# Turn, routing and norm of a tile inside the next tile's products, and twelve early rounds of the token choice, in an encoder layer on one core

## The chip, the cores and the metric

The kernel is one program on one core of a Trainium2 chip. The metric is the device time of one execution in microseconds. The core has five engines with a queue each: PE (TensorE, matrix products into PSUM), DVE (VectorE), ACT (ScalarE), POOL (GpSimd) and SP (SyncE, which issues most transfers). They wait for each other through semaphores: an instruction counts one up when it is done, and a later one, usually on another engine, waits for a value.

## The reference, cut to what matters

Two sequences (1024 and 512 rows of 1024 values) go through an input norm and one layer:

```python
proj = jnp.einsum('bsd,df->bsf', x, w_in)
pool_out = _pool_mixer(proj[..., :o1], w_pool, pool_scale)
attn_out = _mla(...)                                  # 8 heads, softmax attention
mix = jnp.einsum('bsm,md->bsd', jnp.concatenate([pool_out, attn_out], axis=-1), w_o)
x = _layer_norm(DEEPNORM_ALPHA * x + mix, ln1_g, ln1_b)
aff = jax.nn.softmax(jnp.einsum('td,de->te', xt, w_router), axis=-1)
gate, idx = lax.top_k(aff.T, cap)                     # 16 experts, cap 128 and 64 tokens
h = jax.nn.silu(xe @ w_gate) * (xe @ w_up);  ye = (h @ w_down) * gate
x = _layer_norm(DEEPNORM_ALPHA * x + scatter_add(ye), ln2_g, ln2_b)
```

Each expert takes the tokens that have the highest affinity to it, so no expert can start before the affinities of all tokens of a sequence are known.

## The kernel before, in words

Four stages follow each other: projection (0 to 217 us of the span), attention (217 to 575), mixing (575 to 796) and experts with the last norm (from 796). Between stages all engines meet. Inside a stage the order on each engine is the order in which the code is written; nothing reorders it.

**Attention** starts with blocks of keys and queries. On VectorE, `maximum(0, 0)` (L1005, the row maximum of the first scores) stands behind a wait for `u_stored`: the last store of uT must have left the buffer that later takes the heads' outputs (`divide`, L1028). Behind the first maximum comes `rotate(0, 1)` (L995), which needs the second half of the table of angles, `q_table`.

**Mixing** takes twelve tiles of 128 rows, eight of them of the long sequence. Every engine runs `step(s)` for s = 0 to 13; s = 2 to 5 are a hardware loop. For tile s, PE makes `pool_product` (w_pool, into the PSUM bank `ps_t[0]`) a step ahead, and eight `output_slices`, six products of 512 columns each, into `ps_mix[s % 2]`. VectorE adds the residual (L1638, counted by `summed`), takes mean and variance (L1642, L1648), and with the deviation from POOL (L1481, L1483) subtracts and scales (L1650), then multiplies by the gain (L1653). POOL adds the bias (L1487, counted by `x1_done`). ACT writes the scaled copy `acc` (L1532). PE turns the finished rows into `ps_t` (L1790) at the end of step s + 1, when the next tile's slices are done, and routes them (L1761) in step s + 2 behind four slices. The logits are turned (L1776), a softmax runs over VectorE and ACT (L1624, L1535, L1627, L1630), the affinities are turned (L1796) and copied into the lists' rows (L1669).

The parts that PE multiplies are split in two numbers: ACT rounds (`mix_hi`, L1506 for attention's four slices, L1510 for the pool's), VectorE takes the rest (`mix_lo`, L1560 and L1565). The attention part is first scaled by the softmax sums (`scale_attention`, L1556). The turn of a tile's rows waits for three counts: `x1_done`, `t_copied`, and `pool_lo_done` of the tile ahead, as the pool product uses the same bank.

**The token choice** finds a list's values eight at a time: a round is a maximum of eight (L1593), their replacement (L1598) and their positions (L1601). `EARLY_TOPK` gives, per step, how many rounds of the long sequence run ahead (before, after) of the norm; `JOIN`, ten, is their sum. Then come wide rounds for all lists and narrow ones for the short sequence (`PROMPT_FIRST`), in all `JOIN` + 8. VectorE copies positions and values into `lists` (L1700, L1702), PE turns them, and the choice of both halves is merged.

**Experts**: for each of 16 experts PE turns four pairs of gathered rows (L2252), ACT and VectorE split them (`x_lo_done`), and `gate_up` starts once all four pairs are split (L2268).

Of the kernel before, what the change touches and what calls it, by code (L numbers as in the profile page):

```python
# [18 lines left out]
P = 128  # L19
D = 1024  # L20
S_SAMPLE, S_PROMPT = 1024, 512
# [640 lines left out]
def phase_attention(nc, ident, dram, late, handed):  # L662

    with ExitStack() as ctx:
# [305 lines left out]
        def _(dve):  # L970
# [72 lines left out]
            dve.wait_ge(late.u_stored, 16 * N_TILES // 2)  # L1043
# [261 lines left out]
def phase_mix(nc, ident, dram, route, experts, late, first_rows):  # L1305

    with ExitStack() as ctx:
# [53 lines left out]
        topk_step, lists_turned, lists_copied = m.sem("c_topk_step"), m.sem("c_lists_turned"), m.sem("c_lists_copied")  # L1361
        merge_step, half_known = m.sem("c_merge_step"), m.sem("c_half_known")
# [138 lines left out]
        def _(act):  # L1501
# [17 lines left out]

            def step(s, slot=None):  # L1520
# [12 lines left out]
                if has(s, 2):  # L1533
                    act.wait_ge(r_max_done, s - 1)
                    act.activation(e_logits[:, :], ps_a[:, 0:N_EXPERTS], ACT.Exp, bias=neg_max[:, :],  # L1535
                                   accum_out=e_sum[:, :]).then_inc(r_exp_done, 1)
                if has(s, 1):
                    for h in range(2):
                        if has(s, 2):
# [3 lines left out]
                                       ACT.Copy).then_inc(t_copied, 1)  # L1543

            steps(act, step)
            act.wait_ge(wo_done, N_TILES)
            for c in range(experts.EARLY):
                act.wait_ge(experts.loaded[c], 16)
                act.activation(experts.hi[c][:, :], experts.raw[c], ACT.Copy).then_inc(experts.hi_done, 1)

        @block.vector
        def _(dve):
# [54 lines left out]
            def early_topk(s, part):  # L1607
                if isinstance(s, int) and s in EARLY_TOPK:
                    if part == 1 and s == N_TILES - 3:
# [5 lines left out]
            def step(s, slot=None):  # L1615
                slot = s % 2 if slot is None else slot
                if has(s, -1) and not (isinstance(s, int) and s + 1 >= N_TILES):
                    rest_attention(s + 1, 1 - slot)
                    rest_pool(s + 1, 1 - slot)
                early_topk(s, 0)  # L1620
# [4 lines left out]
                if has(s, 2):  # L1625
# [4 lines left out]
                    nc.vector.tensor_scalar(affinity[:, rows_of(s - 2)], e_logits[:, :], e_inv[:, :], None, ALU.mult).then_inc(r_aff_done, 1)  # L1630
                if has(s, 0):
# [11 lines left out]
                    if not isinstance(s, int) or s >= 2:  # L1643
# [5 lines left out]
                    dve.wait_ge(rstd_done, s + 1)  # L1649
                    nc.vector.tensor_scalar(x1[:, slot, :], x1[:, slot, :], moments[:, slot, 0:1], rstd[:, slot:slot + 1],  # L1650
                                            ALU.subtract, ALU.mult).then_inc(centred, 1)
                    dve.wait_ge(centred, s + 1)
                    nc.vector.tensor_tensor(x1[:, slot, :], x1[:, slot, :], ln_g[:, :], ALU.mult).then_inc(scaled, 1)  # L1653
                    if isinstance(s, int) and s == N_TILES - 1:
                        dve.wait_ge(x1_done, s)
                        dve.wait_ge(scaled, s + 1)
                        nc.vector.tensor_tensor(x1[:, slot, :], x1[:, slot, :], ln_b[:, :], ALU.add).then_inc(x1_done, 1)
                if has(s, 2):
                    dve.wait_ge(aff_turned, s - 1)
                    rows = rows_of(s - 2)  # L1660
                    if rows == quarter(0):
                        to = affT[rows, bass.ds((s - 2) * P, P)]
                    elif rows == quarter(1):
                        at = (s - 2) * P - HALF_SAMPLE
                        to = affT[rows, at:at + P]
                    else:
                        at = (s - 2 - SAMPLE_TILES) % 2 * P
                        to = left[(JOIN - 1) % 2][rows, at:at + P]
                    nc.vector.tensor_copy(to, ps_a[rows, P:2 * P]).then_inc(aff_copied, 1)  # L1669
# [17 lines left out]
            found = slice(PROMPT_FIRST, PROMPT_FIRST + CAP_PROMPT)  # L1687
            for x, source in enumerate((index, value)):
                for part in range(4):
                    rows = quarter(part)  # L1690
                    got = source[rows, 0:CAP_SAMPLE] if part < 2 else source[rows, found]
                    if part % 2:
                        got = got[:, ::-1]
                    to = lists[rows, x, :]
                    if part >= 2:
                        got = got.unsqueeze(1).to_broadcast([N_EXPERTS, 2, CAP_PROMPT])
                        to = to.rearrange("p (a c) -> p a c", a=2)
# [706 lines left out]
```

## Time and profile before

| what | value |
|---|---|
| time, median of 3 runs | 1306.43 us (1303.58 to 1306.99) |
| profiled execution, its own time | 1306.65 us |
| its span, first to last instruction | 1304.8 us |
| busy PE / DVE / ACT / POOL | 1169.1 / 921.6 / 687.1 / 377.1 us |
| mean granted clock of PE | 0.96 of full speed |

The table's busy times are sums over the whole span, and the stages have different limits: a full engine in one stage says nothing of the next. In rows of a timeline the columns are the start and the length in microseconds, the engine, the line of the kernel, the instruction with what it writes and reads, its shape and how many were merged; a bracket at the end gives how long the engine had been idle and what released it.

### The profile page before, as it was taken

The numbers are of one execution on the slowest core, as the hardware profiler recorded it, in microseconds if no ns is written. First come the engines' busy times: TensorE is split into PE (matmuls) and PEld (weight loads), VectorE is DVE, ScalarE is ACT, GpSimd is POOL, SyncE is SP. The second block draws the span as 40 slices with busy tenths as digits, with TensorE's granted clock in tenths as the row PEclk, the third lists the DMA queues.
The fourth block names the chain that finished last, engine by engine and source line by source line (L and its number), as shares of the span: only waits on it lengthen the run. The fifth ranks groups of instructions, "written<-read, shape, count | busy, mean of one in ns | idle before, by whom it ended". The sixth has DMA issues, their size and how long they took to land. (4 is left out here: it accounts for less than half of the span.)

```text
span 1304.8 us, 21729 instructions
## 1 busy us (share of the span) xinstructions
PE 1169.1 (90%) x7322; PEld 1054.1 (81%) x7322; DVE 921.6 (71%) x1538; ACT 687.1 (53%) x1191; POOL 377.1 (29%) x437
## 2 busy tenths in 40 slices
PE   5999998789999999989999925999999999999960
PEld 4999997678888888877888715999999999999950
DVE  7655534587877788776566884777777777777738
ACT  4222223566666666662222233667766666776636
POOL 1322210256430000002222132333444343334317
PEclk9999999999999999989999956999999999999985
DMA  8244476832321013038555715888888888888738
GB/s 302 87 165 164 147 240 224 252 119 87 96 64 50 8 35 118 13 107 236 180 162 168 252 65 187 264 274 273 261 280 276 271 289 278 266 255 283 209 83 335
DMA packets 161363, 242.24 MB, mean 186 GB/s; under 512 B 13248, under 2 KB 123424, under 8 KB 161312
## 3 DMA queue, kind: packets, MB, share of 16 engines
q1 hardware_dynamic: 151456, 206.97, 47.4%
q0 software_dynamic: 9856, 34.61, 10.1%
q8 instruction: 29, 0.48, 0.1%
q14 instruction: 22, 0.18, 0.0%
HBM read 179.37 MB, written 62.18 MB: 185 GB/s over the span
## 5 line engine op out<-in xcount | busy, mean ns | idle before, releaser
L2263 PE MATMUL ps_gate_up<-xT_hi_lo,w_hi 128*128 128x384 f32 x896 | 262.9, 357 | 1.4 <-DVE xT_hi_lo L2192 1.4
L2264 PE MATMUL ps_gate_up<-xT_hi_lo,w_lo 128*128 128x192 f32 x896 | 225.2, 251 | 0.0
L2264 PEld LDWEIGHTS ps_gate_up<-xT_hi_lo,w_lo 128*128 128x128 f32 x896 | 171.6, 192 | 0.6
L2263 PEld LDWEIGHTS ps_gate_up<-xT_hi_lo,w_hi 128*128 128x128 f32 x896 | 169.6, 189 | 2.4 <-issue 1.7
L2187 DVE TENSOR_TENSOR w_lo<-w_raw,w_hi 128x2048 fp32r<-128x2048 f32 x63 | 143.8, 2282 | 0.0
L1005 DVE TENSOR_REDUCE neg_max<-ps_scores 128x1 f32<-128x1024 f32 (+1 forms) x80 | 97.7, 1221 | 49.2 <-PE ps_scores L76 48.5
L905 ACT ACTIVATE pT_hi<-ps_probsT 128x512 fp32r<-128x512 f32 x160 | 87.1, 596 | 72.6 <-PE ps_probsT L1134 72.2
L2127 ACT ACTIVATE w_hi<-w_raw 128x2048 fp32r<-128x2048 f32 x62 | 118.4, 1910 | 0.0
L2044 POOL TENSOR_TENSOR d_wait_carrier<-d_zero 128x1 f32<-128x1 f32 x78 | 37.3, 478 | 274.2 <-PE ps_xT L2253 144.7
L1017 DVE TENSOR_TENSOR pT_lo<-ps_probsT,pT_hi 128x512 fp32r<-128x512 f32 x160 | 101.5, 674 | 4.4 <-ACT pT_hi L905 4.3
L914 ACT ACTIVATE probs<-ps_scores,neg_max 128x1024 f32<-128x1024 f32 (+1 forms) x96 | 93.5, 979 | 20.6 <-DVE neg_max L1005 20.3
L1134 PEld LDWEIGHTS ps_probsT<-ident,probs 128*128 128x128 f32 x640 | 73.5, 141 | 29.8 <-DVE pT_lo L1017 14.2
L1134 PE MATMUL ps_probsT<-ident,probs 128*128 128x128 f32 x640 | 84.8, 276 | 14.0 <-ACT probs L914 10.8
L74 PE MATMUL ps_mix<-w_hi,mix_hi 128*128 128x512 f32 x192 | 79.9, 416 | 2.6 <-DVE mix_lo L1565 1.4
L76 PE MATMUL ps_mix<-w_hi,mix_lo 128*128 128x512 f32 x192 | 76.6, 399 | 0.0
L75 PE MATMUL ps_mix<-w_lo,mix_hi 128*128 128x512 f32 x192 | 76.5, 398 | 0.0
L74 PE MATMUL ps_scores<-k_hi,w_in_hi_then_latents 128*128 128x512 f32 x160 | 64.9, 406 | 4.3 <-DVE w_in_lo_then_latents L999 3.1
L2187 DVE TENSOR_TENSOR w_lo<-hen_windows_then_w_o_raw,w_hi 128x2048 fp32r<-128x2048 f32 x30 | 68.6, 2285 | 0.0
L75 PE MATMUL ps_scores<-k_lo,w_in_hi_then_latents 128*128 128x512 f32 x160 | 63.4, 396 | 0.0
L76 PE MATMUL ps_scores<-k_hi,w_in_lo_then_latents 128*128 128x512 f32 x160 | 63.0, 394 | 0.0
L2209 DVE TENSOR_TENSOR hen_windows_then_w_o_raw<-ps_gate_up,gate_rest 128x192 f32<-128x192 f32 x64 | 22.9, 357 | 56.3 <-ACT gate_rest L2144 54.2
L76 PE MATMUL ps_lat<-w_in_hi_then_latents,x0T_lo 128*128 128x384 f32 (+1 forms) x192 | 61.4, 320 | 0.0
(311 smaller groups left out, 3246.5 us busy)
## 6 DMA issues: line engine op xcount, KB each, us to landing
w_raw<-in_w_down SPq DMA_DIRECT2D x32, 1024.0 KB, 6.2
hen_windows_then_w_o_raw<-in_w_gate SPq DMA_DIRECT2D x16, 1024.0 KB, 5.4
hen_windows_then_w_o_raw<-in_w_up SPq DMA_DIRECT2D x16, 1024.0 KB, 5.4
w_raw<-in_w_gate SPq DMA_DIRECT2D x16, 1024.0 KB, 10.3
w_raw<-in_w_up SPq DMA_DIRECT2D x16, 1024.0 KB, 9.2
scratch_x<-x SPq DMA_DIRECT2D x24, 512.0 KB, 2.7
scratch_v<-v_out SPq DMA_DIRECT2D x12, 512.0 KB, 5.8
v_hi_lo<-scratch_v SPq DMA_DIRECT2D x8, 768.0 KB, 4.7
```

The lines of the kernel that those rows point to most:

```text
L74: nc.tensor.matmul(out, a_hi, b_hi, start=first, stop=False)
L75: nc.tensor.matmul(out, a_hi, b_lo, start=False, stop=False)
L76: return nc.tensor.matmul(out, a_lo, b_hi, start=False, stop=last)
L905: act.activation(pT_hi[unit % 2][half_place(n, h)], ps_t[h][:, :].rearrange("p (k t) -> p k t", t=P), ACT.Copy).then_inc(t_hi_done, 1)
L914: last = act.activation(probs[:, n % 2, x * width:(x + 1) * width], ps_s[n % 2][:, x * width:(x + 1) * width], ACT.Exp, bias=neg_max[:, n ...
L1005: nc.vector.tensor_reduce(neg_max[:, n % 2, 0:count], ps_s[n % 2][:, :].rearrange("p (x c) -> p x c", x=count), op=ALU.max, axis=AX.X, neg ...
L1017: nc.vector.tensor_tensor(pT_lo[unit % 2][at], ps_t[h][:, :].rearrange("p (k t) -> p k t", t=P), f32(pT_hi[unit % 2][at]), ALU.subtract).t ...
L1134: last = nc.tensor.transpose(ps_t[h][:, k * P:(k + 1) * P], probs[:, n % 2, (4 * h + k) * P:(4 * h + k + 1) * P], ident[:, :])
L2127: act.activation(w_hi[c][:, :], raw[c], ACT.Copy).then_inc(hi_done, 1)
L2187: nc.vector.tensor_tensor(w_lo[c][:, :], raw[c], f32(w_hi[c][:, :]), ALU.subtract).then_inc(lo_done, 1)
L2263: nc.tensor.matmul(ps[:, 0:2 * N], w_hi[chunk][:, at], xT[:, k, :], start=k == 0, stop=False)
L2264: nc.tensor.matmul(ps[:, 0:N], w_lo[chunk][:, at], xT[:, k, 0:N], start=False, stop=False)
```

## The change: what it does

- Attention: the wait for `u_stored` moves from ahead of the first maximum to the first `divide`.
- Mixing, PE: the turn of a tile's rows moves forward, behind the sixth slice of the next tile; routing (behind the seventh) and the turn of the logits follow in the same step instead of the next one. The turn of the affinities moves to behind the fourth slice.
- Mixing, VectorE: the softmax of a tile comes first in a step, then the rests of the next tile's two parts, then the copy of the affinities, then the early rounds, then the norm.
- Norm: VectorE subtracts the mean and multiplies by the gain in one instruction that doesn't need the deviation; ACT multiplies by the deviation; POOL adds the bias as before. In the last tile VectorE does the last two in one instruction.
- Token choice: three early rounds in each of steps 9 to 12, ahead of the sum; twelve in place of ten. ACT copies the four parts of the values into the lists.
- ACT splits the first two weight chunks of the first expert in step 12 instead of after the steps.
- Experts: the first gate product waits for each pair where it is used, not for all four.

```diff
                 b = unit // 2
+                if unit == 0:
+                    dve.wait_ge(late.u_stored, 16 * N_TILES // 2)
...
             rest_keys(0, (1, 2))
-            dve.wait_ge(late.u_stored, 16 * N_TILES // 2)
 
...
-        EARLY_TOPK = {N_TILES - 3: (0, 2), N_TILES - 2: (1, 2), N_TILES - 1: (1, 1), N_TILES: (0, 3), N_TILES + 1: (0, 0)}
+        EARLY_TOPK = {N_TILES - 3: (3, 0), N_TILES - 2: (3, 0), N_TILES - 1: (3, 0), N_TILES: (3, 0), N_TILES + 1: (0, 0)}
         JOIN = sum(a + b for a, b in EARLY_TOPK.values())
         PROMPT_FIRST = 8 * JOIN
-        TOPK_STEPS = 3 * (JOIN + PROMPT_ROUNDS) - 1 + 8
+        TOPK_STEPS = 3 * (JOIN + PROMPT_ROUNDS) - 1 + 4
...
                 if has(s, 2):
-                    act.wait_ge(logits_done, s - 1)
-                    act.activation(logitsT[:, :], ps_r[:, 0:P], ACT.Copy).then_inc(logits_copied, 1)
+                    act.wait_ge(r_max_done, s - 1)
+                    act.activation(e_logits[:, :], ps_a[:, 0:N_EXPERTS], ACT.Exp, bias=neg_max[:, :],
+                                   accum_out=e_sum[:, :]).then_inc(r_exp_done, 1)
+                if has(s, 1) and not (isinstance(s, int) and s == N_TILES):
+                    act.wait_ge(rstd_done, s)
+                    act.wait_ge(centred, s)
+                    act.activation(x1[:, 1 - slot, :], x1[:, 1 - slot, :], ACT.Copy, scale=rstd[:, 1 - slot:2 - slot]).then_inc(scaled, 1)
+                if isinstance(s, int) and s == N_TILES:
+                    for c in range(2):
+                        split_expert(c)
...
-                if has(s, 2):
-                    act.wait_ge(r_max_done, s - 1)
-                    act.activation(e_logits[:, :], ps_a[:, 0:N_EXPERTS], ACT.Exp, bias=neg_max[:, :],
-                                   accum_out=e_sum[:, :]).then_inc(r_exp_done, 1)
...
+                    act.wait_ge(logits_done, s)
+                    act.activation(logitsT[:, :], ps_r[:, 0:P], ACT.Copy).then_inc(logits_copied, 1)
...
+            for c in range(2, experts.EARLY):
+                split_expert(c)
+            act.wait_ge(topk_step, TOPK_STEPS - 4 - 1)
+            for part in range(4):
+                act.activation(list_row(1, part), found_in(value, part), ACT.Copy).then_inc(values_listed, 1)
...
-                if has(s, -1) and not (isinstance(s, int) and s + 1 >= N_TILES):
-                    rest_attention(s + 1, 1 - slot)
-                    rest_pool(s + 1, 1 - slot)
-                early_topk(s, 0)
...
+                if has(s, -1) and not (isinstance(s, int) and s + 1 >= N_TILES):
+                    rest_attention(s + 1, 1 - slot)
+                    rest_pool(s + 1, 1 - slot)
+                if has(s, 2):
+                    dve.wait_ge(aff_turned, s - 1)
...
+                    nc.vector.tensor_copy(to, ps_a[rows, P:2 * P]).then_inc(aff_copied, 1)
+                early_topk(s, 0)
...
-                    dve.wait_ge(rstd_done, s + 1)
-                    nc.vector.tensor_scalar(x1[:, slot, :], x1[:, slot, :], moments[:, slot, 0:1], rstd[:, slot:slot + 1],
-                                            ALU.subtract, ALU.mult).then_inc(centred, 1)
-                    dve.wait_ge(centred, s + 1)
-                    nc.vector.tensor_tensor(x1[:, slot, :], x1[:, slot, :], ln_g[:, :], ALU.mult).then_inc(scaled, 1)
+                    dve.wait_ge(stats_done, s + 1)
+                    nc.vector.scalar_tensor_tensor(out=x1[:, slot, :], in0=x1[:, slot, :], scalar=moments[:, slot, 0:1], in1=ln_g[:, :],
...
-                        nc.vector.tensor_tensor(x1[:, slot, :], x1[:, slot, :], ln_b[:, :], ALU.add).then_inc(x1_done, 1)
...
+                        dve.wait_ge(rstd_done, s + 1)
+                        dve.wait_ge(centred, s + 1)
+                        nc.vector.scalar_tensor_tensor(out=x1[:, slot, :], in0=x1[:, slot, :], scalar=rstd[:, slot:slot + 1], in1=ln_b[:, :],
+                                                       op0=ALU.mult, op1=ALU.add).then_inc(x1_done, 1)
...
-                    pe.wait_ge(t_copied, 2 * (s - 1))
-                    for k in range(KD):
...
+                    pe.wait_ge(r_aff_done, s - 1)
+                    rows = slice(0, rows_of(s - 2).stop)
+                    nc.tensor.transpose(ps_a[rows, P:2 * P], affinity[:, rows], ident[:, :]).then_inc(aff_turned, 1)
...
-                if has(s, 2):
-                    pe.wait_ge(aff_copied, s - 2)
...
                 if has(s, 1):
                     pe.wait_ge(x1_done, s)
...
-                if has(s, 2):
-                    pe.wait_ge(r_aff_done, s - 1)
-                    rows = slice(0, rows_of(s - 2).stop)
-                    nc.tensor.transpose(ps_a[rows, P:2 * P], affinity[:, rows], ident[:, :]).then_inc(aff_turned, 1)
+                if has(s, 0):
+                    output_slices(s, slot, range(6, 7))
...
+                if has(s, 1):
+                    pe.wait_ge(t_copied, 2 * s)
+                    for k in range(KD):
...
+                if has(s, 0):
+                    output_slices(s, slot, range(7, KD)).then_inc(wo_done, 1)
+                if has(s, 1):
+                    if not isinstance(s, int) or s >= 2:
+                        pe.wait_ge(aff_copied, s - 1)
+                    pe.wait_ge(logits_copied, s)
+                    nc.tensor.matmul(ps_a[:, 0:N_EXPERTS], logitsT[:, :], add_groups[:, :], start=True, stop=True).then_inc(logits_turned, 1)
...
+            pe.wait_ge(values_listed, 4)
...
+                    if e is not None and k < 4:
+                        pe.wait_ge(x_lo_done, 4 * e + k + 1)
...
-                pe.wait_ge(x_lo_done, 4 * e + 4)
...
-                    gate_or_up(ps_g, GATE[f // 2], f, g_done)
+                    gate_or_up(ps_g, GATE[f // 2], f, g_done, e if f == 0 else None)
```

Where this puts the work is shown by the order of instructions on two engines. A row gives the line, the operation, what it writes and reads, its shape and, in brackets, the semaphores that it waits for. Semaphores are numbers that each stage uses anew, and a row may give one the name that it had in an earlier stage: `a_filled` is here `r_aff_done`, `a_kv_stored` is `aff_copied`, `a_kr_stored` is `aff_turned`.

First PE around step 10 of mixing (`ps_x1T` is the bank `ps_t`, in which the rows are turned, and `x1T` its copy, `ps_affinity` the bank of the turned logits and affinities). Before, from the end of the tile ahead to the routing and the turn of the logits:

```order
L74 MATMUL ps_mix<-w_hi,mix_hi 128x512 [waits c_summed,c_mix_lo_done]
...
L1761 MATMUL ps_router<-x1T,w_router 32x128 [waits c_t_copied]
...
L1728 MATMUL ps_x1T<-d,aw_then_windows_then_w_o_raw 128x128 [waits c_d_loaded1]
...
L74 MATMUL ps_mix<-w_hi,mix_hi 128x512 [waits c_logits_copied,a_kv_stored]
...
L1776 MATMUL ps_affinity<-add_groups,logitsT 128x16
...
L1790 MATMUL ps_x1T<-ident,x 128x128 [waits c_pool_lo_done,c_t_copied,c_x1_done]
...
L1796 MATMUL ps_affinity<-ident,affinity 80x128 [waits a_filled]
```

Now:

```order
L74 MATMUL ps_mix<-w_hi,mix_hi 128x512 [waits c_summed,c_mix_lo_done]
...
L1777 MATMUL ps_affinity<-ident,affinity 80x128 [waits a_filled]
L1745 MATMUL ps_x1T<-d,aw_then_windows_then_w_o_raw 128x128 [waits c_d_loaded1]
...
L1792 MATMUL ps_x1T<-ident,x 128x128 [waits c_pool_lo_done,c_t_copied,c_x1_done]
...
L1804 MATMUL ps_router<-x1T,w_router 32x128 [waits c_t_copied]
...
L1813 MATMUL ps_affinity<-add_groups,logitsT 128x16 [waits c_logits_copied,a_kv_stored]
```

Before, the turn of the rows closes a step, and their routing comes a step later behind four slices. Now the rows are turned behind the sixth slice of the next tile, routed behind the seventh, and their logits turned behind the eighth, all in one step; the turn of the affinities comes behind four slices in place of the step's end.

Next VectorE in that step. Before, from the early rounds to the copy of the affinities:

```order
L1630 TENSOR_SCALAR affinity<-e_logits,e_inv 128x16 [waits a_kr_stored,c_r_inv_done]
L1638 SCALAR_TENSOR_TENSOR x<-x_again,ps_mix 128x1024 [waits c_x0_loaded1,c_x1_stored1,c_wo_done,c_acc_done,c_t_done]
...
L1648 BN_AGGR ln_moments<-ln_stats 128x2
L1650 TENSOR_SCALAR x<-x,ln_moments,ln_rstd 128x1024 [waits c_rstd_done]
L1653 TENSOR_TENSOR x<-x,ln_g_all 128x1024 [waits c_centred]
L1669 COPY affT_sample<-ps_affinity 16x128 [waits a_kr_stored]
L1556 TENSOR_TENSOR mix_raw<-mix_raw,inv_rows 128x512 [waits c_inv_loaded1,c_mix_loaded1]
L1593 MAX topk_value<-affT_sample 48x8 [waits a_kv_stored]
...
L1560 TENSOR_TENSOR mix_lo<-mix_raw,mix_hi 128x512 [waits c_mix_hi_done]
L1565 TENSOR_TENSOR mix_lo<-ps_x1T,mix_hi 128x512 [waits c_pool_hi_done]
```

Now:

```order
L1647 TENSOR_REDUCE router_neg_max<-ps_affinity 128x1 [waits c_r_exp_done,c_logits_turned]
...
L1653 TENSOR_SCALAR affinity<-e_logits,e_inv 128x16 [waits a_kr_stored,c_r_inv_done]
L1587 TENSOR_TENSOR mix_lo<-mix_raw,mix_hi 128x512 [waits c_mix_hi_done]
L1592 TENSOR_TENSOR mix_lo<-ps_x1T,mix_hi 128x512 [waits c_pool_hi_done]
L1668 COPY affT_sample<-ps_affinity 16x128 [waits a_kr_stored]
L1620 MAX topk_value<-affT_sample 48x8 [waits a_kv_stored]
...
L1677 SCALAR_TENSOR_TENSOR x<-x_again,ps_mix 128x1024 [waits c_x0_loaded1,c_x1_stored1,c_wo_done,c_acc_done,c_t_done]
...
L1687 BN_AGGR ln_moments<-ln_stats 128x2
L1689 SCALAR_TENSOR_TENSOR x<-x,ln_moments,ln_g_all 128x1024 [waits c_stats_done]
L1583 TENSOR_TENSOR mix_raw<-mix_raw,inv_rows 128x512 [waits c_inv_loaded1,c_mix_loaded1]
```

Softmax and copy now stand ahead of the early rounds and of the sum, the norm has one instruction over the tile in place of two, and nothing but the scaling of the next attention part follows it.

## Rows read from the trace of the kernel before

**Rows 1.** Windows, mid mixing: busy us of PE, PEld, DVE, ACT, POOL; clock.

```profile
656.00:670.00 14.00, 14.00 (x85) 11.34 (x83) 8.22 (x15) 3.91 (x8) 3.72 (x4) 1.00 0.54 169
```

**Rows 2.** Timeline of PE, one tile: start us, length us, engine, line, instruction.

```profile
663.52 1.03 PE L1790 MATMUL ps_x1T<-ident,x 128*128 128x128 f32 x8
...
664.42 0.48 PE L74 MATMUL ps_mix<-w_hi,mix_hi 128*128 128x512 f32 x1
...
670.07 0.64 PE L1761 MATMUL ps_router<-x1T,w_router 128*32 128x128 f32 x16
670.64 1.16 PE L1728 MATMUL ps_x1T<-d,hen_windows_then_w_o_raw 128*128 128x128 f32 x8
671.55 0.47 PE L74 MATMUL ps_mix<-w_hi,mix_hi 128*128 128x512 f32 x1
```

**Rows 3.** Timeline of DVE in the same tile and into the next.

```profile
663.82 1.22 DVE L1638 SCALAR_TENSOR_TENSOR x<-x_again,ps_mix 128x1024 f32<-128x1024 f32 x1 [0.54 <-PE ps_mix L76]
...
666.40 0.20 DVE L1648 BATCH_NORM_AGGREGATE ln_moments<-ln_stats 128x2 f32<-128x12 f32 x1
...
669.73 0.67 DVE L1556 TENSOR_TENSOR mix_raw<-mix_raw,inv_rows 128x512 f32<-128x512 f32 x1
671.61 1.59 DVE L1560 TENSOR_TENSOR mix_lo<-mix_raw,mix_hi 128x512 fp32r<-128x512 f32 x1 [1.20 <-ACT mix_hi L1506]
673.12 0.68 DVE L1565 TENSOR_TENSOR mix_lo<-ps_x1T,mix_hi 128x512 fp32r<-128x512 f32 x1
676.09 0.17 DVE L1624 TENSOR_REDUCE router_neg_max<-ps_affinity 128x1 f32<-128x16 f32 x1 [2.30 <-PE ps_affinity L1776]
...
676.90 0.23 DVE L1630 TENSOR_SCALAR affinity<-e_logits,e_inv 128x16 f32<-128x16 f32 x1
```

**Rows 4.** Timeline of POOL there, the bias of two tiles.

```profile
669.69 2.95 POOL L1487 TENSOR_TENSOR x<-x,ln_b_all 128x1024 f32<-128x1024 f32 x1 [2.19 <-DVE x L1653]
...
683.67 2.37 POOL L1487 TENSOR_TENSOR x<-x,ln_b_all 128x1024 f32<-128x1024 f32 x1 [2.19 <-DVE x L1653]
```

**Rows 5.** Timeline of ACT there, one pass over a tile.

```profile
672.74 1.06 ACT L1532 ACTIVATE acc_out<-x 128x1024 f32<-128x1024 f32 x1 [0.30 <-POOL x L1487]
```

**Rows 6.** Timeline of DVE in the expert stage, a split of weights.

```profile
844.05 2.28 DVE L2187 TENSOR_TENSOR w_lo<-w_raw,w_hi 128x2048 fp32r<-128x2048 f32 x1
```

**Rows 7.** Timeline of POOL then, a one-element operation.

```profile
844.56 1.83 POOL L2044 TENSOR_TENSOR d_wait_carrier<-d_zero 128x1 f32<-128x1 f32 x1 [6.33 <-DMA scratch_acc<-y_prompt_rows,scatter_at]
```

**Rows 8.** Timeline of DVE, the sums of tiles 0, 1, 8 and 11.

```profile
596.71 1.21 DVE L1638 SCALAR_TENSOR_TENSOR x<-x_again,ps_mix 128x1024 f32<-128x1024 f32 x1
...
608.47 1.22 DVE L1638 SCALAR_TENSOR_TENSOR x<-x_again,ps_mix 128x1024 f32<-128x1024 f32 x1 [1.86 <-PE ps_mix L76]
...
705.39 1.22 DVE L1638 SCALAR_TENSOR_TENSOR x<-x_again,ps_mix 128x1024 f32<-128x1024 f32 x1 [0.54 <-PE ps_mix L76]
...
750.45 1.22 DVE L1638 SCALAR_TENSOR_TENSOR x<-x_again,ps_mix 128x1024 f32<-128x1024 f32 x1 [0.35 <-PE ps_mix L76]
```

**Rows 9.** Timeline of DVE, last softmax to the lists.

```profile
768.40 0.17 DVE L1624 TENSOR_REDUCE router_neg_max<-ps_affinity 128x1 f32<-128x16 f32 x1
...
770.32 0.70 DVE L1593 MAX8 topk_value<-topk_left 112x8 f32<-112x512 f32 x1
...
782.68 0.42 DVE L1593 MAX8 topk_value<-topk_left 48x8 f32<-48x256 f32 x1
...
783.95 0.42 DVE L1593 MAX8 topk_value<-topk_left 48x8 f32<-48x256 f32 x1
...
785.92 0.97 DVE L1700 COPY topk_lists<-topk_value 16x128 f32<-16x128 f32 x4
```

**Rows 10.** Timeline of DVE at the start of attention.

```profile
233.65 1.22 DVE L1005 TENSOR_REDUCE neg_max<-ps_scores 128x1 f32<-128x1024 f32 x1 [5.87 <-PE ps_scores L76]
238.73 0.69 DVE L995 TENSOR_TENSOR q_work<-ps_q,q_table 128x512 f32<-128x512 f32 x1 [3.86 <-DMA q_table<-in_q_table]
```

**Rows 11.** Timeline of PE at the first expert's first product.

```profile
801.00 0.66 PE L2263 MATMUL ps_gate_up<-xT_hi_lo,w_hi 128*128 128x384 f32 x1 [1.36 <-DVE xT_hi_lo L2192]
```

More of the change, by code:

```diff
@@ L1368, in phase_mix, with found_in, list_row @@
         ROUNDS, PROMPT_ROUNDS = CAP_SAMPLE // 8, CAP_PROMPT // 8
-        EARLY_TOPK = {N_TILES - 3: (0, 2), N_TILES - 2: (1, 2), N_TILES - 1: (1, 1), N_TILES: (0, 3), N_TILES + 1: (0, 0)}
+        EARLY_TOPK = {N_TILES - 3: (3, 0), N_TILES - 2: (3, 0), N_TILES - 1: (3, 0), N_TILES: (3, 0), N_TILES + 1: (0, 0)}
         JOIN = sum(a + b for a, b in EARLY_TOPK.values())
         PROMPT_FIRST = 8 * JOIN
-        TOPK_STEPS = 3 * (JOIN + PROMPT_ROUNDS) - 1 + 8
+        TOPK_STEPS = 3 * (JOIN + PROMPT_ROUNDS) - 1 + 4
+        def found_in(source, part):
+            rows = quarter(part)
+            got = source[rows, 0:CAP_SAMPLE] if part < 2 else source[rows, PROMPT_FIRST:PROMPT_FIRST + CAP_PROMPT]
+            if part % 2:
+                got = got[:, ::-1]
+            return got if part < 2 else got.unsqueeze(1).to_broadcast([N_EXPERTS, 2, CAP_PROMPT])
+        def list_row(x, part):
+            to = lists[quarter(part), x, :]
+            return to if part < 2 else to.rearrange("p (a c) -> p a c", a=2)
         block = ctx.enter_context(nc.Block())
@@ L1518, in _, with split_expert @@
                     round_attention(0, 0)
+            def split_expert(c):
+                act.wait_ge(wo_done, N_TILES)
+                act.wait_ge(experts.loaded[c], 16)
+                act.activation(experts.hi[c][:, :], experts.raw[c], ACT.Copy).then_inc(experts.hi_done, 1)
             def step(s, slot=None):
@@ L1608, in early_topk @@
                 if isinstance(s, int) and s in EARLY_TOPK:
-                    if part == 1 and s == N_TILES - 3:
+                    if part == 0 and s == N_TILES - 3:
                         dve.wait_ge(aff_copied, SAMPLE_TILES)
@@ L1630, in step @@
                     nc.vector.tensor_scalar(affinity[:, rows_of(s - 2)], e_logits[:, :], e_inv[:, :], None, ALU.mult).then_inc(r_aff_done, 1)
+                if has(s, -1) and not (isinstance(s, int) and s + 1 >= N_TILES):
[3 more added lines that the diff above has]
+                    dve.wait_ge(aff_turned, s - 1)
+                    rows = rows_of(s - 2)
+                    if rows == quarter(0):
+                        to = affT[rows, bass.ds((s - 2) * P, P)]
+                    elif rows == quarter(1):
+                        at = (s - 2) * P - HALF_SAMPLE
+                        to = affT[rows, at:at + P]
+                    else:
+                        at = (s - 2 - SAMPLE_TILES) % 2 * P
+                        to = left[(JOIN - 1) % 2][rows, at:at + P]
+                    nc.vector.tensor_copy(to, ps_a[rows, P:2 * P]).then_inc(aff_copied, 1)
+                early_topk(s, 0)
                 if has(s, 0):
@@ L1686, in _ @@
             dve.wait_ge(topk_step, n)
[L1687 to L1697, printed above, removed]
-                    start = (0, HALF_SAMPLE, S_SAMPLE, S_SAMPLE + HALF_PROMPT)[part]
-                    if x or not part:
-                        nc.vector.tensor_copy(to, got).then_inc(topk_step, 1)
-                    else:
-                        nc.vector.tensor_scalar(to, got, float(start), None, ALU.add).then_inc(topk_step, 1)
-            assert n + 8 == TOPK_STEPS
+            for part, first_token in enumerate((0, HALF_SAMPLE, S_SAMPLE, S_SAMPLE + HALF_PROMPT)):
+                to, got = list_row(0, part), found_in(index, part)
+                if part == 0:
+                    nc.vector.tensor_copy(to, got).then_inc(topk_step, 1)
+                else:
+                    nc.vector.tensor_scalar(to, got, float(first_token), None, ALU.add).then_inc(topk_step, 1)
+            assert n + 4 == TOPK_STEPS
             dve.wait_ge(lists_turned, 1)
@@ L1769, in step @@
                     output_slices(s, slot, range(4, 6))
-                if has(s, 2):
-                    pe.wait_ge(aff_copied, s - 2)
-                    pe.wait_ge(logits_copied, s - 1)
-                if has(s, 0):
-                    output_slices(s, slot, range(6, 7))
-                if has(s, 2):
-                    nc.tensor.matmul(ps_a[:, 0:N_EXPERTS], logitsT[:, :], add_groups[:, :], start=True, stop=True).then_inc(logits_turned, 1)
-                if has(s, 0):
-                    output_slices(s, slot, range(7, KD)).then_inc(wo_done, 1)
-                if isinstance(s, int) and s == 1:
-                    pe.wait_ge(ln_loaded, 48)
-                    pe.wait_ge(groups_step, GROUPS - 1)
                 if has(s, 1):
```

32 lines of the change are left out of this document (10 added, 22 removed).

## The prediction

> **What bounds the kernel now.** I read the windows first. In the middle of the mixing stage PE is busy for all 14.00 us of a 14 us stretch at full clock, VectorE for 8.22, ScalarE for 3.91, GpSimd for 3.72 [rows 1]. So between tile 1 and tile 8 a tile costs what PE's products cost: seven tiles from 608.47 to 705.39, 13.85 us each [rows 8]. Then I read the timelines of one tile, since the change moves waits and not work. PE turns the finished rows of the tile before right behind a tile's last product (663.52), and routes them only after four slices of the following tile (670.07) [rows 2]. That leaves nearly a tile for the norm, the bias and the softmax. The end of the stage is the reverse: from the last tile's sum at 750.45 to the first joint round of the token choice at 770.32, and on to the lists, VectorE decides [rows 8, 9]. In the expert stage PE is the bound again, and it waits once, 1.36 us before its first product [rows 11].
>
> **The change part by part.** Times T below count from a tile's sum on VectorE (663.82 in the trace).
>
> *VectorE's early wait.* The first row maximum of attention starts at 233.65 after 5.87 us of idling, which is put down to PE; the wait for the stored uT that the change moves stands just there. But next VectorE rotates a query block, and that waits 3.86 us for the q_table load, until 238.73 [rows 10]. The second maximum stands behind this rotation in both kernels, and the load hangs on nothing that VectorE does. The first maximum then comes 5.6 us sooner and the queue stops at the same 238.73. Bounds 0 and -5.6; I take 0.
>
> *The loop, where the turn moves forward.* The new PE order asks for three things inside a tile: the affinities after four slices; the finished rows after six; and, as the transposes share a PSUM bank with the pool product, the rest of the next tile's pool part. No engine has more work, so the cost is what comes late.
>
> The affinities: statistics end at T 2.78 (666.60), the new fused product at 1.22 (the sum's length, same form) brings 4.0, scaling the attention part 0.67 brings 4.7, and softmax from maximum to affinities takes 1.04 (676.09 to 677.13) [rows 3]; with handovers, T 5.85. PE starts the tile at T -0.3 and needs 5.65 us for four slices (664.42 to 670.07), plus a small turn of the logits [rows 2]: ready at 5.5. It waits about 0.4.
>
> The transposes: ScalarE's new scaling stands behind the softmax's exponential in its queue, so it starts at about 5.4 and ends, at 1.06 for a pass [rows 5], at 6.5. Its reader is the bias on GpSimd: 2.37 us when undisturbed [rows 4], so to 8.9. Now VectorE's rest of the attention part becomes ready near 7.1 and falls inside the bias. In the trace that meeting is seen: the bias ran 669.69 to 672.64 [rows 4], the rest started at 671.61, took 1.59 and ended 0.56 after the bias, where the same size of two SBUF inputs took 0.67 [rows 3]. So the rest ends at 9.5, the pool part's rest 0.6 later, and PE has its permission at 10.2. Without any of this PE would be there at 5.5 + 0.91 for the pool product (670.64 to 671.55) + 2.83 for two slices [rows 2] = 9.25. The two waits are one sum, as the second swallows the first: 0.95. One more thing lengthens it: GpSimd's two small operations for the deviation start beside the fused product, which reads two SBUF tensors. A one-element operation took 1.83 us on GpSimd while such a product ran, and ended with it [rows 6, 7]. Held behind the product and the scaling, the deviation comes near 5.5 and shifts the scaling by up to 0.25. Bounds 0.4 and 1.2 per tile; I take 1.0, seven times: +7.0 (2.8 to 8.4).
>
> The page "SBUF — State Buffer" of the Trainium skill, section "Who interferes with whom", has a rule that speaks against this change: a VectorE instruction with two SBUF inputs and a GpSimd instruction that reads SBUF exclude each other, and whichever was issued second blocks for all of the first. The trace agrees, with the 1.59 for 0.67 and the 1.83 above. By that rule the loop's term is the +7.0; if the engines only shared, it would be the +2.8.
>
> *Tile 1.* Before, from the sum of tile 0 to that of tile 1 are 11.76 us [rows 8], since nothing is turned or routed in it. Now both are: 0.90 (663.52 to 664.42) and 0.57 (670.07 to 670.64) [rows 2], 1.5 in all, and a wait at the transposes, where PE is ready at 8.95 and the permission comes between 8.75 and 10.3. +2.8 (1.5 to 2.9).
>
> *Three early rounds in each of tiles 9 to 12.* A round costs 2.06 us: six take from 770.32 to 782.68 [rows 9]. Three stand behind the pool part's rest and ahead of the next sum, so a tile lasts 10.15 + 0.3 for the copy + 6.2 = 16.6, and VectorE is the bound. For the last one nothing is left to scale: the affinities are early, rows are finished at 8.6, then 0.9 + 1.4 + 0.6 + 1.4 + 0.3 of PE give 13.2. Together 46.4 against 45.06 from tile 8 to tile 11 [rows 8]: +1.3 (0.9 to 1.8).
>
> *From the last sum to the joint rounds.* Before 19.87. Now the second fused product ends at 4.0 + 0.85 of waiting for the deviation + 1.2 = 6.1; softmax, turn and copy of tile 10 take 1.92 (768.40 to 770.32) [rows 9], three rounds 6.2, and again 1.92: 16.1. ScalarE rounds two chunks in the meantime (four passes' worth, 4.2 us), then the tile's copies, so the routing is at most 0.7 late: 16.8. -3.1 (-2.0 to -3.8).
>
> *Rounds and lists.* Twelve early rounds for ten: four wide joint rounds in place of six, four narrow ones (1.27, 782.68 to 783.95) in place of two: -2 x (2.06 - 1.27) = -1.6. The four copies of values, 0.97 [rows 9], go to ScalarE, which starts them half a round earlier: -1.0 (0 to -1.0).
>
> *The first gate product* no longer waits for the fourth pair. PE's 1.36 [rows 11] go, since three pairs arrive while it works: -1.4 (-1.0 to -1.4). The three added waits per expert are long met and cost nothing, at most some hundredths each.
>
> Sum: 2.8 + 7.0 + 1.3 - 3.1 - 1.6 - 1.0 - 1.4 = +4.0. The profiled execution took 1306.65 us for a span of 1304.8, 0.2 above the median of 1306.43, so I add it to the execution: 1310.7. All lower ends together give -2.6 (the early wait apart), all upper ends +8.5.
>
> **The rivals.** *VectorE is not held* (the other side): the rest of the attention part runs beside the bias. It decides if its record has its 0.67 although the bias is running. Then only the 0.4 for the affinities stays per tile (+2.8), tile 1 costs 1.5, a tile with rounds 7.1 + 0.67 + 0.6 to the end of the pool part's rest, then 0.3 + 6.2, 14.9 in all, so 43.0 for the last three, -2.1, and with the -7.1 of the end: -4.9, 1301.8. Against it stands [rows 3, 4]; for it, that the order of arrival could turn where tiles slip.
>
> *Half the wait*: the deviation isn't held, handovers are short, and a tile costs 0.5 more: +0.5, 1307.2. For it: my terms are a few tenths each.
>
> *No wait at all*: the affinities too are in time: -7.7, 1299. Against it: VectorE's queue of known durations.
>
> *The early wait is worth its 5.6*: then -1.6, 1305. Against it: the q_table load [rows 10].
>
> **How the numbers follow.** Forecast 0.53, own range 1309 to 1315, half the wait 0.22, not held 0.15, no wait 0.05, early wait 0.05. A measurement of this kernel can tell about 0.3% (3.9 us). The forecast lies just above that line, so 0.05 of it counts as no change: slower 0.48, same 0.32 (with half the wait and the early wait), faster 0.20. The range 1301 to 1316 leaves out the case without any wait and the upper tail.
>
> **What would show it.** Right: from tile 2 to tile 8 sums 14.6 to 15.1 us apart; PE idle ahead of the transposes with the pool part's rest as releaser, and ahead of the turned affinities; VectorE's rest of the attention part at 1.5 to 2.5 us, ending about 0.6 after the bias; sums of tiles 9 and 10 about 16.6 apart with VectorE never idle ahead of them; 16 to 17 from the last sum to the joint rounds; the second maximum of attention still right behind the q_table. Wrong: sums 13.9 apart, a rest of 0.7 under a running bias, or a second maximum before 238.

## The result, and the profile after

The changed kernel took 1316.83 us (median of 4 runs, 1315.03 to 1319.82) against 1305.74 for the kernel before (4 runs, 1303.58 to 1306.99): a ratio of 1.0083, interval 1.0067 to 1.0100, so about 11 us slower. The profiled execution has a span of 1313.1 us and a time of 1315.03, 8.4 above that of before. The forecast of slower was right; the time lies 0.8 above its range.

The sums of tiles 0, 1, 8 and 11 on VectorE, as in [rows 8]:

```profile
596.20 1.21 DVE L1677 SCALAR_TENSOR_TENSOR x<-x_again,ps_mix 128x1024 f32<-128x1024 f32 x1
...
611.01 1.22 DVE L1677 SCALAR_TENSOR_TENSOR x<-x_again,ps_mix 128x1024 f32<-128x1024 f32 x1 [4.87 <-PE ps_mix L76]
...
714.28 1.22 DVE L1677 SCALAR_TENSOR_TENSOR x<-x_again,ps_mix 128x1024 f32<-128x1024 f32 x1 [4.59 <-PE ps_mix L76]
...
760.65 1.22 DVE L1677 SCALAR_TENSOR_TENSOR x<-x_again,ps_mix 128x1024 f32<-128x1024 f32 x1 [1.01 <-PE ps_mix L76]
```

Tile 1 takes 14.81 for 11.76, the seven tiles of the loop 14.75 each for 13.85, tiles 9 to 11 together 46.37 for 45.06. Next come the last softmax and the joint rounds, which answer [rows 9]. VectorE first:

```profile
774.92 0.17 DVE L1647 TENSOR_REDUCE router_neg_max<-ps_affinity 128x1 f32<-128x16 f32 x1 [0.18 <-PE ps_affinity L1813]
775.53 0.16 DVE L1650 RECIPROCAL e_inv<-e_sum 128x1 f32<-128x1 f32 x1 [0.43 <-ACT e_logits L1544]
775.72 6.98 DVE L1653 TENSOR_SCALAR affinity<-e_logits,e_inv 128x16 f32<-128x16 f32 x1
783.25 0.30 DVE L1668 COPY topk_left<-ps_affinity 16x128 f32<-16x128 f32 x1 [0.56 <-PE ps_affinity L1777]
783.59 0.69 DVE L1620 MAX8 topk_value<-topk_left 112x8 f32<-112x512 f32 x1
...
796.61 0.21 DVE L1717 CAST topk_lists<-topk_index 16x128 f32<-16x128 uint32 x1
```

And GpSimd, ScalarE and PE of the same stretch:

```profile
767.07 3.70 ACT L1538 ACTIVATE w_hi<-hen_windows_then_w_o_raw 128x2048 fp32r<-128x2048 f32 x2
...
769.05 9.17 POOL L1507 TENSOR_TENSOR w_lo<-hen_windows_then_w_o_raw,w_hi 128x2048 fp32r<-128x2048 f32 x2 [3.74 <-ACT w_hi L1538]
...
775.39 3.70 ACT L1538 ACTIVATE w_hi<-w_raw 128x2048 fp32r<-128x2048 f32 x2
...
778.11 4.56 POOL L1507 TENSOR_TENSOR w_lo<-w_raw,w_hi 128x2048 fp32r<-128x2048 f32 x1
...
782.75 0.46 PE L1777 MATMUL ps_affinity<-ident,affinity 128*112 128x128 f32 x1 [7.87 <-DVE affinity L1653]
797.63 0.69 PE L1819 MATMUL ps_router<-ident,topk_lists 128*128 128x128 f32 x2 [14.42 <-DVE topk_lists L1719]
...
810.07 0.67 PE L2283 MATMUL ps_gate_up<-xT_hi_lo,w_hi 128*128 128x384 f32 x1
```

The multiplication of 128x16 elements that makes the last affinities (L1653) took 6.98 us, where it took 0.23 in [rows 3]. It ended at 782.70, and the third of GpSimd's splits of the first expert's weights (L1507, two in the one row, one in the other) ended at 782.67. No other instruction of any engine ends there. Behind the multiplication stand PE, the copy and the joint rounds.

In the kernel before, the lists begin and are turned at

```profile
784.92 0.21 DVE L1700 CAST topk_lists<-topk_index 16x128 f32<-16x128 uint32 x1
...
786.94 0.69 PE L1801 MATMUL ps_router<-ident,topk_lists 128*128 128x128 f32 x2 [16.99 <-DVE topk_lists L1700]
```

Set against before by stretches of the two spans, in us:

| stretch | before | after | difference | predicted |
|---|---|---|---|---|
| start to the first sum | 596.71 | 596.20 | -0.5 | 0 |
| tile 1 | 11.76 | 14.81 | +3.05 | +2.8 |
| tiles 2 to 8 | 96.92 | 103.27 | +6.35 | +7.0 |
| tiles 9 to 11 | 45.06 | 46.37 | +1.3 | +1.3 |
| last sum to joint rounds | 19.87 | 22.94 | +3.1 | -3.1 |
| joint rounds | 14.60 | 13.02 | -1.6 | -1.6 |
| lists | 2.02 | 1.02 | -1.0 | -1.0 |
| turn of the lists to first gate product | 14.06 | 12.44 | -1.6 | -1.4 |
| from there to the end | 503.80 | 503.03 | -0.8 | 0 |
| sum | 1304.8 | 1313.1 | +8.3 | +4.0 |

Every term but one came out within 0.8 us. That one is off by 6.2. The table accounts for the 8.3 between the two profiled executions; the medians are 11.1 apart, in a repeat 8.4 (the last experiment), and where the other 2.7 lie isn't shown.

Inside the loop one tile shows the two waits. PE's turn of the affinities and of the rows [rows 2]:

```profile
645.50 0.39 PE L76 MATMUL ps_mix<-w_hi,mix_lo 128*128 128x512 f32 x1
646.09 0.28 PE L1777 MATMUL ps_affinity<-ident,affinity 128*16 128x128 f32 x1 [0.19 <-DVE affinity L1653]
...
649.67 0.39 PE L76 MATMUL ps_mix<-w_hi,mix_lo 128*128 128x512 f32 x1
650.27 1.09 PE L1792 MATMUL ps_x1T<-ident,x 128*128 128x128 f32 x8 [0.21 <-DVE mix_lo L1592]
```

VectorE's rest of the attention part, and GpSimd's bias, which answer [rows 3, 4]:

```profile
646.68 2.39 POOL L1502 TENSOR_TENSOR x<-x,ln_b_all 128x1024 f32<-128x1024 f32 x1 [1.79 <-ACT x L1549]
...
647.15 2.46 DVE L1587 TENSOR_TENSOR mix_lo<-mix_raw,mix_hi 128x512 fp32r<-128x512 f32 x1 [1.12 <-ACT mix_hi L1521]
649.54 0.68 DVE L1592 TENSOR_TENSOR mix_lo<-ps_x1T,mix_hi 128x512 fp32r<-128x512 f32 x1
```

The rest took 2.46 and ended at 649.61, 0.54 after the bias (649.07). Products follow each other here every 0.227 us, so PE was ready for the two turns at 645.73 and 649.90 and lost about 0.37 ahead of either.

At the start of attention [rows 10], the first maximum came 4.9 us sooner, and VectorE's queue stopped at the q_table load all the same:

```profile
228.77 1.22 DVE L1005 TENSOR_REDUCE neg_max<-ps_scores 128x1 f32<-128x1024 f32 x1
237.07 0.69 DVE L995 TENSOR_TENSOR q_work<-ps_q,q_table 128x512 f32<-128x512 f32 x1 [7.08 <-DMA q_table<-in_q_table]
237.68 1.21 DVE L1005 TENSOR_REDUCE neg_max<-ps_scores 128x1 f32<-128x1024 f32 x1
```

### The profile page after: what moved, and what is told of

It reads as the page before. It is cut to its first block and busy times, and to the rows that moved or that the text cites. A ratio compares the mean times of both kernels' runs of the same rounds, so it can differ in the third digit from the quotient of the medians.

```text
span 1313.1 us, 21797 instructions
## 1 busy us (share of the span) xinstructions
PE 1171.7 (89%) x7322; PEld 1051.5 (80%) x7322; DVE 925.8 (71%) x1532; ACT 699.8 (53%) x1206; POOL 385.5 (29%) x437
## 5 line engine op out<-in xcount | busy, mean ns | idle before, releaser
L2062 POOL TENSOR_TENSOR d_wait_carrier<-d_zero 128x1 f32<-128x1 f32 x78 | 40.0, 513 | 269.5 <-PE ps_xT L2271 141.7
```

## The experiments

Theory: two holds of VectorE by GpSimd make the loss, the small one in every tile and a large one at the last softmax, which the sum had not priced. Rivals: the stall is ScalarE's or a fetch of instructions; and the loop grows because PE's new order is longer by itself. Each ratio is to runs of the kernel before on the same chip, whose medians were 1307.67, 1308.54 and 1308.99.

**Take the stalled instruction off VectorE.** In ScalarE's last step, with VectorE's own multiplication of this tile left out:

```diff
+                    if isinstance(s, int) and s == N_TILES + 1:
+                        act.wait_ge(r_inv_done, s - 1)
...
+                        act.activation(affinity[:, rows_of(s - 2)], e_logits[:, :], ACT.Copy, scale=e_inv[:, :]).then_inc(r_aff_done, 1)
```

> The changed kernel, but the last tile's affinities (e_logits times e_inv) are computed by ScalarE behind its exponential; VectorE's multiplication of that tile is gone. Theory (VectorE's multiplication of two SBUF operands stood from 775.72 to 782.70 because GpSimd's three splits of the first expert's weights, 769.05 to 782.67, hold a port that it needs): the last softmax ends about 6.5 us sooner, 16.2 to 16.6 from the last sum to the joint rounds in place of 22.9, and the time falls from 1316.8 to about 1310.2. GpSimd's splits stay where they are. Rival (something else held VectorE there, say a fetch of instructions or ScalarE's split): the next VectorE instruction stands instead, and the time stays within 1 us of 1316.8.

Measured: 1310.62, ratio 1.0030 (1.0018 to 1.0043); last sum to joint rounds 16.27. ScalarE multiplies and VectorE goes on while GpSimd splits:

```profile
768.53 9.14 POOL L1507 TENSOR_TENSOR w_lo<-hen_windows_then_w_o_raw,w_hi 128x2048 fp32r<-128x2048 f32 x2 [3.73 <-ACT w_hi L1538]
...
775.22 0.31 ACT L1550 ACTIVATE affinity<-e_logits,e_inv 128x16 f32<-128x16 f32 x1 [0.23 <-DVE e_inv L1655]
...
776.08 0.30 DVE L1674 COPY topk_left<-ps_affinity 16x128 f32<-16x128 f32 x1 [0.89 <-PE ps_affinity L1783]
776.41 0.69 DVE L1625 MAX8 topk_value<-topk_left 112x8 f32<-112x512 f32 x1
...
777.61 4.55 POOL L1507 TENSOR_TENSOR w_lo<-w_raw,w_hi 128x2048 fp32r<-128x2048 f32 x1
```

The stall is gone and did not move to the next VectorE instruction, so a fetch of instructions is out.

**Leave the instruction, move GpSimd.**

```diff
             steps(pool, step)
+            pool.wait_ge(r_aff_done, N_TILES)
```

> The changed kernel, but GpSimd starts its splits of the first expert's weights only when the last tile's affinities are there; ScalarE's two early splits stay in step 12. Theory (GpSimd holds VectorE): the multiplication takes 0.23 again, the joint rounds begin 16.2 to 16.6 after the last sum, and GpSimd's 13.7 us end beside the end of the rounds; 1310.2, up to 1 us more if they meet the additions of the lists. Rival (ScalarE's split, which also ran then, holds VectorE): the multiplication still takes 3 to 7 us, and the time stays at 1313 to 1317.

Measured: 1311.37, ratio 1.0028 (1.0015 to 1.0040), 16.22 from the last sum to the joint rounds. The multiplication:

```profile
778.05 0.23 DVE L1654 TENSOR_SCALAR affinity<-e_logits,e_inv 128x16 f32<-128x16 f32 x1
...
778.37 9.01 POOL L1508 TENSOR_TENSOR w_lo<-hen_windows_then_w_o_raw,w_hi 128x2048 fp32r<-128x2048 f32 x2 [10.74 <-DVE affinity L1654]
787.35 4.50 POOL L1508 TENSOR_TENSOR w_lo<-w_raw,w_hi 128x2048 fp32r<-128x2048 f32 x1
```

ScalarE's splits ran where the change put them (one pair began at 777.72, ahead of the multiplication), so they are not the cause.

**Make the stall in the kernel before**, by ScalarE's early splits alone (`split_expert` holds the lines that stood behind the steps):

```diff
+                if isinstance(s, int) and s == N_TILES:
+                    for c in range(2):
+                        split_expert(c)
```

> The kernel before, with one edit of the change alone: ScalarE splits the first two weight chunks of the first expert at the end of step 12. Theory: GpSimd starts its splits about 763.7 in place of 770.85, so VectorE's last multiplication of the softmax (769.2) meets them; if GpSimd's instructions hold the port back to back it stands until the third ends near 777.4, +8 us, 1314; if the port comes free between two, until 772.8, +3.6, 1309.4. Rival (the stall needs the new order of VectorE or of the norm): no change, 1305.7.

Measured: 1311.44, ratio 1.0032 (1.0016 to 1.0048); last sum to joint rounds 23.15 for 19.87.

```profile
766.43 9.03 POOL L1492 TENSOR_TENSOR w_lo<-hen_windows_then_w_o_raw,w_hi 128x2048 fp32r<-128x2048 f32 x2 [9.39 <-ACT w_hi L1523]
...
771.99 3.51 DVE L1637 TENSOR_SCALAR affinity<-e_logits,e_inv 128x16 f32<-128x16 f32 x1
...
775.43 4.50 POOL L1492 TENSOR_TENSOR w_lo<-w_raw,w_hi 128x2048 fp32r<-128x2048 f32 x1
```

One edit of seven makes a stall in an otherwise unchanged kernel. Here VectorE came through at the border of the second and third split (775.46), the smaller of the two forecasts, though the time is 2 us above what was expected for it; in the changed kernel it was held across that border in two executions (6.98, 6.94), and in a variant of it below (6.94).

**Read the tensor from PSUM**, to see what is held. In the last tile ScalarE writes the exponentials there (its edit isn't shown), and VectorE's edit, its lines cut at the right, is

```diff
-                    nc.vector.tensor_scalar(affinity[:, rows_of(s - 2)], e_logits[:, :], e_inv...
+                    of = ps_a[:, 32:32 + N_EXPERTS] if isinstance(s, int) and s == N_TILES + 1 else e_logits[:, :]
+                    nc.vector.tensor_scalar(affinity[:, rows_of(s - 2)], of, e_inv...
```

> The changed kernel, but in the last tile ScalarE writes the exponentials into PSUM and VectorE's multiplication reads them there (its factor e_inv and its result stay in SBUF); GpSimd's and ScalarE's splits are where the change put them. Theory (what is held is a multiplication that reads its tensor from SBUF, as the Trainium skill's page on SBUF says of tensor_scalar in a mode of two ports): it takes 0.2 to 0.3 in the middle of GpSimd's split, 16.3 from the last sum to the joint rounds, about 6.5 us below the changed kernel (1310). Rival (the factor that is read from SBUF, or the write to SBUF, is what is held): it stands 6 to 7 us as before, 1316.8.

Measured: 1311.73, ratio 1.0022 (1.0005 to 1.0038), 16.2 from the last sum (760.93) to the joint rounds. In the middle of GpSimd's splits:

```profile
769.33 9.12 POOL L1507 TENSOR_TENSOR w_lo<-hen_windows_then_w_o_raw,w_hi 128x2048 fp32r<-128x2048 f32 x2 [3.73 <-ACT w_hi L1538]
...
776.01 0.23 DVE L1655 TENSOR_SCALAR affinity<-ps_affinity,e_inv 128x16 f32<-128x16 f32 x1
...
777.13 0.69 DVE L1621 MAX8 topk_value<-topk_left 112x8 f32<-112x512 f32 x1
...
778.36 4.57 POOL L1507 TENSOR_TENSOR w_lo<-w_raw,w_hi 128x2048 fp32r<-128x2048 f32 x1
```

The same multiplication with the same factor and result runs in 0.23. So its tensor in SBUF is what made it wait.

**The loop: no bias on GpSimd.** ScalarE's scaling and GpSimd's bias are gone; in their place stands, behind the softmax on VectorE, for the tile before:

```diff
+                    nc.vector.scalar_tensor_tensor(out=x1[:, 1 - slot, :], in0=x1[:, 1 - slot, :], scalar=rstd[:, 1 - slot:2 - slot], in1=ln_b[:, :],
+                                                   op0=ALU.mult, op1=ALU.add).then_inc(x1_done, 1)
```

> The changed kernel, but in every tile VectorE multiplies by the deviation and adds the bias in one instruction behind the softmax (as the changed kernel does in the last tile); ScalarE's scaling and GpSimd's bias are gone. Theory (in the loop the rest of the attention part stands 2.46 for 0.68 behind GpSimd's bias, and PE waits for it at the turn): the rest takes 0.68, sums of tiles 2 to 8 stand 14.0 to 14.3 apart in place of 14.75, tiles 9 and 10 about 15.4 in place of 16.6; together -5 to -7, with the stall of the last softmax left in: about 1310.5. Rival (the turn costs PE its time by itself, whatever VectorE does): sums stay 14.7 apart and only the last tiles gain 1 to 2 us, 1315.

Measured: 1305.96, ratio 0.9986 (0.9971 to 1.0002). In the trace the rest takes 0.68, the loop's tiles 14.31, tile 1 13.47 for 14.81, tiles 9 to 11 43.05 for 46.37, and PE's wait ahead of the rows' turn is gone. The stall of the last softmax stays:

```profile
659.60 0.68 DVE L1579 TENSOR_TENSOR mix_lo<-mix_raw,mix_hi 128x512 fp32r<-128x512 f32 x1
...
768.30 6.94 DVE L1645 TENSOR_SCALAR affinity<-e_logits,e_inv 128x16 f32<-128x16 f32 x1
```

These stretches fell by 7.8 together, where 5 to 7 had been expected, and the time lies 4.5 below the 1310.5 expected. The edit took work off the chain of the norm as well as the hold. The changed kernel's own trace tells the two apart: there the bias ended at 649.07, 0.83 before PE was ready for the rows' turn, so the rows were in time; VectorE's rests ended at 650.22, and PE began at 650.27.

**The end alone, on the kernel before**: the value lists on ScalarE and the waits of the gate pairs, as in the change's diff.

> The kernel before with two edits of the change alone: ScalarE copies the four parts of the values into the lists, and the first gate product waits for each pair where it is used. Theory (both are on the path behind the loop, and worth what the sum gave them): the stretch from the lists to the first gate product shortens by 1.0 + 1.4, the time falls by 2 to 2.7 us against the kernel before (ratio about 0.998). Rival (PE only waits later, at the weights or at the second pair): 0 to -1 us.

Measured: 1303.71, ratio 0.9966 (0.9946 to 0.9985); the lists 1.02 for 2.02, the turn to the gate product 12.42 for 14.06. Both terms are there without the rest of the change. The two stretches fell by 2.6; the time fell by more than the 2 to 2.7 expected, 4.8, with an interval from 2.0 to 7.1.

**Both holds away** (the bias on VectorE and the last affinities on ScalarE):

> The changed kernel without either hold by GpSimd: the bias and the deviation on VectorE behind the softmax in every tile, the last tile's affinities on ScalarE. Theory (the two terms are separate and add): 6.5 us below the run with VectorE's bias alone, which was 1.3 us below the kernel before; 7 to 8 us below the kernel before (ratio about 0.994), the last sum to the joint rounds at 16.2. Rival (they overlap, the end of the stage then being bound by ScalarE or PE): 2 to 4 us below the kernel before.

Measured: 1302.99, ratio 0.9961 (0.9945 to 0.9978). The stretch behind the last sum fell from 22.92 to 16.27, as expected. The time lies 5.6 below the kernel before, between the 7 to 8 of the theory and the 2 to 4 of the rival. Set against the run with VectorE's bias alone, on another chip, the time fell by less than the 6.5 expected, 0.0025 of it or 3.3 us, with intervals of 2 us on either side; against the changed kernel on the same chip (1316.92, below) it is 13.9 lower, where the stretches behind the first sum up to the joint rounds fell by 14.5. That speaks for two terms that add. In the profiled execution the stretches that no edit touches, up to the first sum and from the first gate product on, were 2.5 and 1.1 us longer than with VectorE's bias alone.

**Both holds away, and PE's turn of the affinities behind the pool product**:

```diff
+                if has(s, -1) and not (isinstance(s, int) and s + 1 >= N_TILES):
+                    pool_product(s + 1, 1 - slot)
                 if has(s, 2):
                     pe.wait_ge(r_aff_done, s - 1)
...
-                if has(s, -1) and not (isinstance(s, int) and s + 1 >= N_TILES):
-                    pool_product(s + 1, 1 - slot)
```

> As the one without holds, and PE turns the affinities behind the next tile's pool product, not ahead of it. Theory (what is left in the loop is PE's wait for the affinities, 0.2 to 0.4 a tile): sums of tiles 2 to 8 stand 13.9 to 14.1 apart in place of 14.3, 2 to 3 us less than without this edit (ratio about 0.992). Rival (the rest of a tile's growth is PE's products themselves in the new order): sums stay at 14.3, the time that of the run without holds.

Measured: 1299.91, ratio 0.9934 (0.9908 to 0.9959); the loop's tiles 13.88, from the sums of tiles 1 and 8:

```profile
612.24 1.22 DVE L1680 SCALAR_TENSOR_TENSOR x<-x_again,ps_mix 128x1024 f32<-128x1024 f32 x1 [5.85 <-PE ps_mix L76]
...
709.37 1.22 DVE L1680 SCALAR_TENSOR_TENSOR x<-x_again,ps_mix 128x1024 f32<-128x1024 f32 x1 [5.34 <-PE ps_mix L76]
```

The same window as in [rows 1] (busy us of PE, PEld, DVE, ACT, POOL, then the clock, the share of the DMA engines and GB/s), first of the changed kernel, then of this one:

```profile
656.00:670.00 14.00, 13.69 (x82) 10.70 (x81) 7.65 (x14) 4.95 (x9) 4.00 (x3) 1.00 0.51 164
```

```profile
656.00:670.00 14.00, 14.00 (x86) 11.43 (x85) 7.70 (x15) 3.79 (x8) 1.59 (x2) 1.00 0.54 170
```

PE is full again. So of the 0.91 that a tile had grown, 0.45 went with the wait ahead of the rows' turn and 0.42, taken away second, with the one ahead of the affinities'; 0.03 is left for PE's new order by itself. This version beats both kernels, the one before by 8.6 us on that chip.

**The changed kernel once more:**

> The changed kernel once more, for a comparison on the chip of these runs: 9 to 12 us above the kernel before (ratio 1.007 to 1.009), with VectorE's last multiplication again at 6 to 7 us and ending with GpSimd's third split. Rival (that stall was an accident of the one profiled execution): 0.23 and 2 to 5 us above.

Measured: 1316.92 for 1308.54, ratio 1.0066 (1.0040 to 1.0092): 8.4 us, a little under the 9 to 12 expected. The multiplication took 6.94 and ended at 784.12, GpSimd's third split at 784.09:

```profile
777.18 6.94 DVE L1653 TENSOR_SCALAR affinity<-e_logits,e_inv 128x16 f32<-128x16 f32 x1
...
779.59 4.50 POOL L1507 TENSOR_TENSOR w_lo<-w_raw,w_hi 128x2048 fp32r<-128x2048 f32 x1
```

The stall belongs to the kernel.

## Why the prediction was right in sign and wrong in size

- *From the last sum to the joint rounds* is the step that failed. It said: "ScalarE rounds two chunks in the meantime (four passes' worth, 4.2 us), then the tile's copies, so the routing is at most 0.7 late: 16.8. -3.1". It followed those chunks only to ScalarE's own queue, and so put at nothing the wait of VectorE's last multiplication. Their reader is GpSimd, whose splits then began at 769.05 and covered the last softmax. Without the hold the stretch is 16.2 to 16.3 in five kernels, inside the step's own 16.1 to 16.8; the hold adds 6.7. With -3.6 in place of +3.1, the stretches would add up to +1.6.
- That the slowdown is clear of the noise is owed to this hold, which the forecast didn't have, and so the sign is in part luck. In the three kernels that lose only the hold at the end (the multiplication on ScalarE, GpSimd later, the tensor in PSUM) the ratios are 1.0030, 1.0028 and 1.0022, no more than the 0.3% that the prediction itself called the least that can be told.
- In the kernel before, ScalarE's splits stand behind the last exponential, so GpSimd's start behind the multiplication:

```profile
769.20 0.23 DVE L1630 TENSOR_SCALAR affinity<-e_logits,e_inv 128x16 f32<-128x16 f32 x1
...
770.85 9.14 POOL L1492 TENSOR_TENSOR w_lo<-hen_windows_then_w_o_raw,w_hi 128x2048 fp32r<-128x2048 f32 x2 [16.59 <-ACT w_hi L1549]
```

  The first split started 1.65 after the multiplication did; in the changed kernel it starts 6.67 ahead of it. The rows in which VectorE and GpSimd hold each other were at hand [rows 3, 4, 6, 7], and the prediction used them for the loop only.
- It also read the rule of the Trainium skill ("SBUF — State Buffer", "Who interferes with whom") too narrowly, as one on two SBUF inputs. The same section says that copies, casts and `tensor_scalar` can take both ports to SBUF, if their operands allow it, and then contend with GpSimd as well. The runs agree: 6.98 from SBUF, 0.23 from PSUM, under the same split. The rule as the prediction put it ("whichever was issued second blocks for all of the first") doesn't cover all of the 6.98: the multiplication stood since 775.72, ahead of the third split (778.11), and was held through that one too.
- *The loop*: +6.35 for +7.0, 0.907 a tile for 1.0, with the mechanism as worked out (rest 2.46 and 0.54 behind the bias). Its two waits were put down as one sum of 0.95, "as the second swallows the first"; taken away in turn, the rows' first, they are worth 0.45 and 0.42. No run takes away the wait for the affinities alone, so the swallowing isn't tested.
- GpSimd's deviation, put "near 5.5" after a tile's sum, was ready at 4.5 (started at 643.48, 1.40 long where the same step took 0.55 before, after the sum at 640.35). In that tile it delayed nothing; in the last one VectorE waited 0.50 for it (put at 0.85).
- *Tile 1, tiles 9 to 11, rounds, lists, gate product*: right within 0.3.
- *The early wait*: right, 0, though the second maximum, at 237.68, came before the 238 that was to show it wrong. It still stands right behind the load of the q_table, and the load's time varies: the rotation behind it began at 236.9 to 239.4 in the three traces without the move and at 237.1 to 240.8 in the eight with it. The first sum came at 594.8 to 599.8 in the three and at 595.7 to 599.1 in the eight.
- *The rivals*: VectorE was held, so the case on the other side fell; half the wait put a tile at 0.5 more, and it is 0.91. All the chances hung on the loop, and none on the end.

## What to carry to other kernels

When an engine's work is moved earlier, follow it to its readers on other engines, and set what those will now run beside. Of VectorE and GpSimd, list the SBUF tensors that each reads in every stretch where both are busy: here a multiplication of 0.23 us on the path waited for the rest of one GpSimd instruction of about 4.6 us and for the whole of the next. It cost little to avoid: 0.31 us on ScalarE, or 0.23 with the tensor in PSUM.

## What the runs showed of the hardware

- A VectorE multiplication by a per-partition factor (128x16, fp32) waited for GpSimd's `tensor_tensor` on SBUF when its tensor was in SBUF (3.51 to 6.98 us in four executions), and not when it was in PSUM (0.23 in one). In the same stretch `reciprocal` of one column (0.16 at 775.53), the maximum from PSUM (0.17) and the rounds of the token choice (13.02 behind the splits, 13.03 with them alongside) were not held.
- A held instruction came through between two GpSimd instructions back to back in one execution, and was held through both in three. What decides it stays open.
